# Residual squares summed on GpSimd, with output tile 6 first and tile 7 last at seven stage boundaries

## The reference

```python
h = rmsnorm(x, g) * (1 + scale) + shift      # scale, shift, gate come from a matrix times a condition vector
x = x + gate * mixer(h)                      # a half-weighted gate in the first block's feed-forward stages
# rmsnorm(x, g) = x * rsqrt(mean(x*x, axis=-1) + 1e-6) * g
```

## Time and profile before

| | |
|---|---|
| time before, median of 3 runs | 1783.66 us (1782.2 to 1787.7) |
| the profiled execution: its own time | 1789.82 us |
| its span, first to last instruction | 1788.0 us |
| busy share of the span: PE, PE weight loads, DVE, ACT, POOL | 98%, 95%, 81%, 54%, 0% |
| mean granted TensorE clock, as a share of full | 0.996 |

### The profile page before, as it was taken

How to read it: one execution, slowest core, us unless ns; L and a number is a source line. 1 busy time by engine, 2 the same in 40 slices (tenths; PEclk the granted TensorE clock), 3 DMA queues, 4 the chain that set the end, 5 groups by cost and what they waited for, 6 DMA issues and landing times.

```text
span 1788.0 us, 34255 instructions
## 1 busy us (share of the span) xinstructions
PE 1747.4 (98%) x14686; PEld 1698.2 (95%) x14686; DVE 1453.3 (81%) x1749; ACT 958.2 (54%) x1254; POOL 0.2 (0%) x4
## 2 busy tenths in 40 slices
PE   4999999999999999999999999999999999999999
PEld 4999999998999999999999999999999998989999
DVE  7799898888899989897658999765899887567766
ACT  4444566665544454445765333565655556775553
POOL 0000000000000000000000000000000000000000
PEclk9999999999999999999999999999999999999999
DMA  9998744443698959894435979343388535426551
GB/s 394 414 419 330 301 142 165 151 157 141 243 419 330 360 201 387 326 389 177 154 136 220 391 308 356 138 148 139 114 303 289 211 143 179 151 73 214 188 196 37
DMA packets 68150, 426.23 MB, mean 238 GB/s; under 512 B 7489, under 2 KB 10833, under 8 KB 31825
## 3 DMA queue, kind: packets, MB, share of 16 engines
q1 hardware_dynamic: 63936, 416.22, 61.1%
q10 hardware_dynamic: 4112, 8.62, 1.4%
HBM read 423.74 MB, written 3.17 MB: 239 GB/s over the span
## 4 chain that ended last, share of the span: by engine, by line
PE 92%; ACT 3%; DVE 3%; DMA 2%; issue 1%; DVEq 0%; ACTq 0%; SPq 0%
PE bank L1563 24%; PE bank L1564 24%; PE bank L1565 24%; PE bank L1616 2%; PE bank L1618 2%; PE bank L1617 2%; PE bank L1576 1%; PE bank L1672 1%; PE bank L1590 1%; PE bank L1972 1%; DMA mix<-mods 1%; PE bank L1579 1%; ACT w_hi L495 1%; DMA biases<-scratch 1%; PE bank L1806 1%
## 5 line engine op out<-in xcount | busy, mean ns | idle before, releaser
L1563 PE MATMUL bank<-h_hi,w_hi 128*128 128x256 f32 x2504 | 695.4, 278 | 0.9 <-DVE h_lo_rest L1172 0.9
L1564 PE MATMUL bank<-h_lo_rest,w_hi 128*128 128x256 f32 x2504 | 693.7, 277 | 0.0
L1565 PE MATMUL bank<-h_hi,w_lo 128*128 128x256 f32 x2504 | 693.7, 277 | 0.0
L913 DVE TENSOR_TENSOR w_lo<-raw,w_hi 128x2048 fp32r<-128x2048 f32 x267 | 610.2, 2287 | 94.4 <-ACT w_hi L495 93.3
L495 ACT ACTIVATE w_hi<-raw 128x2048 fp32r<-128x2048 f32 x276 | 528.4, 1914 | 157.3 <-PE bank L1565 137.6
L1563 PEld LDWEIGHTS bank<-h_hi,w_hi 128*128 128x128 f32 x2504 | 471.9, 188 | 1.1 <-DVE h_lo_rest L1172 1.1
L1564 PEld LDWEIGHTS bank<-h_lo_rest,w_hi 128*128 128x128 f32 x2504 | 470.2, 188 | 0.0
L1565 PEld LDWEIGHTS bank<-h_hi,w_lo 128*128 128x128 f32 x2504 | 470.1, 188 | 0.0
L1563 PE MATMUL bank<-a_hi,w_hi 128*128 128x256 f32 x1280 | 357.3, 279 | 0.2 <-DVE a_lo L1284 0.2
L1564 PE MATMUL bank<-a_lo,w_hi 128*128 128x256 f32 x1280 | 354.6, 277 | 0.0
L1565 PE MATMUL bank<-a_hi,w_lo 128*128 128x256 f32 x1280 | 354.6, 277 | 0.0
(11 more groups left out here) (299 smaller groups left out, 1998.5 us busy)
## 6 DMA issues: line engine op xcount, KB each, us to landing
raw<-weights SPq DMA_DIRECT2D x276, 1024.0 KB, 5.2
modws<-mods SPq DMA_DIRECT2D x144, 768.0 KB, 6.8
mix<-mods SPq DMA_DIRECT2D x5, 1024.0 KB, 8.8
mix<-mods ACTq DMA_DIRECT2D x8, 512.0 KB, 13.5
biases<-scratch ACTq DMA_DIRECT2D x1, 2048.0 KB, 14.0
mix<-biases ACTq DMA_DIRECT2D x4, 512.0 KB, 4.0
modws<-mods SPq DMA_DIRECT2D x1, 1024.0 KB, 12.2
x<-xin SPq DMA_DIRECT2D x1, 1024.0 KB, 10.9
```

The costliest lines, as they stand in the source:

```text
L913: eng.tensor_tensor(w_lo[g % NW][:, :], raw[g % NRAW][:, :], w_hi[g % NW][:, :], ALU.subtract).then_inc(sems["wlo"], 1)
L1563: eng.matmul(dst, ah, bh, start=start, stop=False, skip_group_check=skip)
L1564: eng.matmul(dst, ah, bl, start=False, stop=False, skip_group_check=skip)
L1565: return eng.matmul(dst, al, bh, start=False, stop=stop, skip_group_check=skip)
```

## The change

`out_order(st)` gives the order of the output tiles in the last block: 6, 0, 1, 2, 3, 4, 5, 7 after stages 0, 2, 3, 4, 6, 7 and 8; the old order elsewhere. There (`six_first`) DVE updates tile 6 alone, then three pairs, then tile 7 alone, and adds no squares. ACT squares in that order. GpSimd, which had no work, adds squares: 0+6, 1+2, those two, +3, and apart from these 4+5. PE makes three products: of the sum of 0, 1, 2, 3 and 6, of 4+5, and of 7. The diff, cut to its core, shows in this order the new function, ACT's squares (`norm`), DVE's `residual`, GpSimd's program, PE's `summed_squares` and PE's `last`:

```diff
+def out_order(st):
+    if st + 1 >= len(STAGES) or STAGES[st] == "mamba" or st + 1 == RESCALED:
+        return tuple(range(KT))
+    return 6, 0, 1, 2, 3, 4, 5, 7
...
-                for m in range(KT):
+                for n, m in enumerate(out_order(st - 1) if st else range(KT)):
                     if st:
-                        k.wait("xup", st - 1, b=m)
+                        k.wait("xup", st - 1, b=n)
...
-                for two in ((0, 1), (2, 3), (4, 5), (6, 7)):
-                    if summed and two[0] == (6 if final else 4):
+                turns = ((6,), (0, 1), (2, 3), (4, 5), (7,)) if six_first(st) else ((0, 1), (2, 3), (4, 5), (6, 7))
+                for n, two in enumerate(turns):
+                    if final and two[0] == 6:
                         add_squares(0, 1)
-                    if summed and two[0] == 6 and not final:
-                        add_squares(2, 3)
-                        add_squares(0, 2)
-                    if two[0] < 6:
-                        k.wait("pair", st, b=two[0] // 2)
+                    if two[-1] < 7:
+                        k.wait("pair", st, b=n)
                     else:
                         eng.wait_ge(sems["blk"], plan.first[st] + NBLK[stages[st]])
...
+        @block.gpsimd
+        def _(eng):
+            k = Steps(eng, plan, sems)
+            def add(st, m, other):
+                k.inc("sqa", eng.tensor_tensor(work3[:, m, :], work3[:, m, :], work3[:, other, :], ALU.add))
+            for st in range(1, NST):
+                if six_first(st - 1):
+                    k.wait("sq", st, b=1)
+                    add(st, 0, 6)
+                    k.wait("sq", st, b=3)
+                    add(st, 1, 2)
+                    k.wait("sqa", st, b=1)
+                    add(st, 0, 1)
+                    k.wait("sqa", st, b=2)
+                    k.wait("sq", st, b=4)
+                    add(st, 0, 3)
+                    k.wait("sq", st, b=6)
+                    add(st, 4, 5)
...
-                order = [(0, 0), (2, 1), 4, 5, 6, 7] if kinds == 2 else [4, 5, (0, 2), 6, 7]
+                order = [(0, 0), (2, 1), 4, 5, 6, 7] if kinds == 2 else [(0, 3), (4, 4), 7]
...
-                for m in range(KT):
+                for m in out_order(st):
...
+                    if m == 7 and six_first(st):
+                        k.wait("xup", st, b=0)
...
-                    if m in (1, 3, 5):
+                    if m in (1, 3, 5) or m == 6 and six_first(st):
                         k.inc("pair", mm)
```

More of the change, by code:

```diff
@@ L123, in score_bank, with six_first @@
     return (5, 6, 7, 4) if i else (4, 5, 6, 7)
+def out_order(st):
+    if st + 1 >= len(STAGES) or STAGES[st] == "mamba" or st + 1 == RESCALED:
+        return tuple(range(KT))
+    return 6, 0, 1, 2, 3, 4, 5, 7
+def six_first(st):
+    return out_order(st)[0] == 6
 def side_list(st):
@@ L186, in steps @@
         g = GROUPS[kind]
-        out = {"fold": 4 if st else 0, "mods": 1, "modv": 1, "pair": 3, "xup": 8, "sq": 8, "ss": 1, "ln": 1, "rstd": 1,
+        out = {"fold": 4 if st else 0, "mods": 1, "modv": 1, "pair": 4 if six_first(st) else 3, "xup": 8, "sq": 8, "ss": 1, "ln": 1, "rstd": 1,
                "t": 8, "hhi": 8, "hlo": 8, "ahi": 0, "alo": 0}
         if st and self.stages[st - 1] != "mamba":
-            out |= {"sqa": 4 if st == RESCALED else 3}
+            out |= {"sqa": 4 if st == RESCALED else 5}
         if st == RESCALED:
@@ L1066, in residual @@
                 nxt = st + 1
-                summed = nxt < NST and not token
                 final = nxt == RESCALED
                 def add_squares(m, other):
[L1071 to L1075, removed]
+                    for r in range(2):
+                        k.wait("sq", nxt, b=2 * other + r)
                         s = sq2 if r else work3
                         k.inc("sqa", eng.tensor_tensor(s[:, m, :], s[:, m, :], s[:, other, :], ALU.add))
-                for two in ((0, 1), (2, 3), (4, 5), (6, 7)):
-                    if summed and two[0] == (6 if final else 4):
+                turns = ((6,), (0, 1), (2, 3), (4, 5), (7,)) if six_first(st) else ((0, 1), (2, 3), (4, 5), (6, 7))
+                for n, two in enumerate(turns):
+                    if final and two[0] == 6:
                         add_squares(0, 1)
-                    if summed and two[0] == 6 and not final:
-                        add_squares(2, 3)
-                        add_squares(0, 2)
-                    if two[0] < 6:
-                        k.wait("pair", st, b=two[0] // 2)
+                    if two[-1] < 7:
+                        k.wait("pair", st, b=n)
                     else:
@@ L1097, in residual @@
                             scalar=modv[:, st, 16 + m:17 + m], in1=x[:, m, :], op0=ALU.mult, op1=ALU.add))
-                if summed and final:
+                if final:
                     add_squares(2, 3)
```

## The result

The changed kernel takes 1809.2 us (median of 4, 1806.3 to 1811.9) against 1785.7 (4 runs, 1782.2 to 1788.6): a ratio of 1.0129, 95% interval 1.0103 to 1.0156, that is 18 to 28 us slower. The forecast was 1795 in a range of 1782 to 1813; the time lies where the rival of the exclusion stood, 1801 to 1813, and outside the 1787 to 1801 of the case that I called likeliest.

What follows compares the result with a forecast made beforehand. PE, busy 98%, bounds the kernel, so only stage ends count. Late sums +5.4 and clock falls +6 make +11.4 us: the median 1783.7 becomes 1795, range 1782 to 1813.

Steps and rivals of the forecast that it cites:

- the rival of the exclusion: At stage ends DVE's w_lo piece and GpSimd's adds shut each other out, plus clock falls: 1801 to 1813 us; chance 0.27.
- the case that I called likeliest: At the seven stage ends, late sums with some falls of PE's clock: 1787 to 1801 us; chance 0.44.
- What bounds, and where to look: PE, busy 98%; only stage ends count, and each moves by as much as the last two products' start, 641.08.
- S, the pace of an add: On GpSimd, time from one add's start to a dependent next one's: 0.76 us taken, even at 0.565.
- The late sums, +5.4: At seven stage ends the last sum reaches PE late: +0.78 us at six, +0.7 after stage 8, together +5.4.
- The exclusion: At stage ends, DVE's two-SBUF-operand w_lo piece and GpSimd's adds run one after the other: +2.5 each, +17.7 in all; chance 0.27.
- The clock: PE's idle time at stage ends drops its clock to half; 1.7 us a fall, about half of seven boundaries, +6.
- the forecast's case: At stage ends, late sums without exclusion, clock falling at about half of the seven: +11.4 us, 1795; chance 0.44.
- the rival's case: At stage ends, exclusion with PE idle 3.7 us and the clock falling at each: +18 and +12, 1813; chance 0.27.
- What was set at nothing: DVE's 21 adds (9 us), two of PE's five products, the wait before tile 7 and GpSimd's start: no effect.
- The wait before tile 7: On PE, the wait for update 6 ahead of tile 7: update ends by 636.1, tile starts at 639.19, no cost.
- GpSimd's start: GpSimd's added ISA row at its start has until the first boundary, past 200 us, so it costs nothing.

Runs made afterwards that it cites:

- e1: Changed kernel, but DVE's 1536-column w_lo piece waits until GpSimd's last add (4+5) is done; 1791.3 us against 1783.4 for the kernel before, ratio 1.0043.
- e3: Changed kernel with the w_lo piece waiting for the last add and 10 unused matmuls ahead of the first product of squares; 1790.7 us, ratio 1.0045.
- e8: Changed kernel without add 4+5, four products on PE, w_lo piece waiting for the last add; ratio 1.0025, four runs 1783.6 to 1785.3 us, six 1794.5 to 1795.9.
- e6: Changed kernel's tile order, five adds and three products, but all adds on DVE and none on GpSimd; 1793.5 us against 1788.0, ratio 1.0028.
- e2: Changed kernel with 24 more unused matmuls on PE between the last output matmul and the first product of squares; 1801.5 us, ratio 1.0099.
- e4: Changed kernel, but DVE's w_lo piece reads PSUM in place of raw, so only one SBUF operand (output not the reference's); 1791.2 us, ratio 1.004.
- e5: Kernel before, its order and five products kept, with only DVE's three adds moved to GpSimd; 1787.7 us against 1788.0, ratio 1.0006.
- e9: Changed kernel's tile order with only three adds on GpSimd and five products on PE, w_lo piece waiting for nothing; 1783.4 us against 1784.7, ratio 0.9996.
- e7: Changed kernel with DVE's 1536-column w_lo piece as three instructions of 512 columns; 1802.3 us against 1788.0, ratio 1.0095.

## Why the prediction came out as it did

The time lies in the stated range only because that range took in the exclusion. The likeliest case, late sums alone, ends 8 us below it: the forecast had the place of the loss and its smaller part, and not its largest.

**What bounds, and where to look: right.** The loss is at the seven stage ends (+19.5 of 23.5 us up to Ln, +22.8 up to the next stage's first product), and it moves as the start of the last two products does: +2.4 there and +2.4 for Ln at the end of stage 2 (3.58 against 1.19, 4.75 against 2.36).

**S, the pace of an add: right.** 0.76 was taken and 0.80 measured (0.73 and 0.07 to the next). The way I got it, operands in turn, is not shown by that. The Trainium skill's price (GPSIMD Engine Reference, Performance versus the Vector engine) gave 0.63 by an estimate; the trace is above it (0.73 for the add, where the estimate has 0.56). A fixed part of each add, which the estimate leaves out, would explain that; only one size ran here, so it is not shown.

**The late sums, +5.4: right, as a term.** It shows alone in e1 and e3: +5.9 and +6.0 on the stage ends, +7.7 and +8.0 by the ratios. e8 shows that it is the length of the chain: one link less, and 4.6 of it are gone. e6 has as much without GpSimd, +5.8 and +5.0, with one fall of the clock in it.

**The exclusion: this is the step that failed.** The forecast let DVE's piece run beside the adds and gave the rival 0.27, for want of any row. It was worked out at +2.5 for an end and +17.7 in all; e2, which has it and no fall of the clock, shows +16.4 on the seven ends and +18.1 in all. e1 and e4 show the cause: take away the time that the two share, or DVE's second SBUF operand, and 10.5 or 9.8 us of the 16.4 are gone. The rule of the Trainium skill (SBUF — State Buffer, Who interferes with whom) says just this, both halves of it: DVE with two SBUF inputs against a GpSimd instruction that reads SBUF, and no contention with one; the trace agrees, with 2.28 us for (0+3) beside the piece and 0.73 beside e4's. I had it before me and should have given it more than even odds. One detail of mine was off: I had (0+3) go first by 0.08 us; the piece was first by 0.04 in the profiled run, and since (4+5) stands behind (0+3) the sum is the same.

**The clock: right in kind, wrong in both sizes.** In the forecast's case, PE idle for 1.3 us, I took a fall at every second end, +6. With PE idle for 1.3 to 2.1 us it fell at none of seven ends in e1 and at one of seven in e4, where it cost 0.9 us. In the rival's case, PE idle for about 3 us, I took a fall at all seven, +12; it fell at six, and cost 6.5 by the traces (5.4 by the times of e2), about 1.1 each and not 1.7. I had priced a fall as if PE had a full block of matmuls to run in it. But each of the six falls was over within 0.5 us of the next stage's first product, so it slowed the products of squares and the unused matmuls, and the block hardly at all.

So the sum, measured to the first product of the next stage, is 5.8 us for the chain (e1), 10.5 for the exclusion (e2 less e1) and 6.5 for the clock (the changed kernel less e2): 22.8 of 23.5 us. The rest is within what the runs scatter.

**What was set at nothing: right, as far as a time can show.** DVE's 21 adds and two products of five were worth nothing: e5 takes only the adds from DVE and gains 1.5 us on the seven ends, below what a time can show, and a product more costs nothing in e8. The wait before tile 7 and GpSimd's start are no part of any chain (e9).

## What to carry to other kernels

Before work goes to an idle engine, write down for each piece when its inputs are there, how long the chain behind the last input is, and when the consumer asks: here the old way asked for a square at 641.08, and four adds after square 2 could not be done by then at any pace above 0.56 us. Then look at what DVE runs at that moment: an instruction of it with two operands in SBUF, and an add of GpSimd, are one behind the other, and a wait, or an operand in PSUM, can save most of the loss. And an idle PE at a stage end can cost twice: unused matmuls in that time gave back 5 to 6 us. Unused matmuls that stand behind a wait do the opposite when the clock has fallen: 14 of them took 3.46 us in place of 2.02, and delayed the next stage.

## What the runs showed of the hardware that was not expected

- The exclusion changes hands after each instruction: with the piece in three, an add waits for one third (1.05 and 1.17 us) and never for two, though DVE's next third was ready (e7).
- An instruction that waits for the other engine is shown as running: 2.28 us for an add of 0.73. Its duration, and not a wait, is where to look for it.
- The one held does not wait for quite the whole of the other: it is longer by 0.12 to 0.16 us less than what was left (the piece 0.44 for 0.56 in the changed kernel, 0.32 for 0.46 in e5), and (0+3) ends 0.57 after the piece, where it takes 0.73 alone.
- Two adds of which the second needs the first stand 0.80 us apart (642.50 to 643.30); without that need they follow at 0.68 (640.03 to 640.71 in e1).
- TensorE can be slower through a whole stage with the same instructions and a granted clock of 1.00: stage 5 of the kernel before takes 186.7 us from its first product to its last output matmul, where the ten other profiles have 181.3 to 181.5, and its matmuls are 281 ns each in place of 276 to 277. In e7 it is stage 2, 186.8 in place of 181.5. That is 5.3 us each time, most of the 6.2 by which the profiled execution of the kernel before lay above the median, and more than the whole effect of e9's or e5's edit. No run here shows why.
